# One statistic of the updated residual from sums taken early, one joint last down phase, and GpSimd adding every chunk

## The reference

```python
def _pre(x, g, mod, k):
    return _rmsnorm(x, g) * (1.0 + mod[:, 3 * k + 1][:, None]) + mod[:, 3 * k][:, None]
def _post(x, y, g, mod, k, weight):
    return x + weight * mod[:, 3 * k + 2][:, None] * _rmsnorm(y, g)
# a sub-layer
x = _post(x, _swiglu(_pre(x, g[0], mod_lat, 0), ffn1_gu[l], ffn1_down[l]), g[1], mod_lat, 0, 0.5)
```

## Time and profile before

| what | value |
|---|---|
| three runs | 2658.7, 2658.51, 2654.53 us; median 2658.51 |
| profiled execution, own time | 2659.8 us |
| its span, first to last instruction | 2658.0 us |
| PE busy | 2593.4 us (98%) |
| DVE busy | 1616.4 us (61%) |
| ACT busy | 714.7 us (27%) |
| POOL busy | 812.6 us (31%) |
| granted TensorE clock, mean | 0.995 |

### The profile page before, as it was taken

The page is one execution under the profiler, slowest core; times in us unless marked ns, Lnnn a source line. Parts: engine busy times, 40 slices in busy tenths (PEclk is TensorE's granted clock), DMA queues, the critical chain, the costliest instruction groups (busy, mean ns, idle before and its releaser), DMA issues.

```text
span 2658.0 us, 40824 instructions
## 1 busy us (share of the span) xinstructions
PE 2593.4 (98%) x17044; PEld 2436.5 (92%) x17044; DVE 1616.4 (61%) x2270; ACT 714.7 (27%) x1050; POOL 812.6 (31%) x1286
## 2 busy tenths in 40 slices
PE   6999999999999999999999999999999999999998
PEld 5999999998989899999999899999999878888886
DVE  6688878767574676676676633433434684544444
ACT  4222212123334411112212412112112424322222
POOL 1278876832140100000001248667551031000001
PEclk9999999999999999999999999999999999999999
DMA  9534544453464234434432422222223575233331
GB/s 336 153 124 157 157 143 134 159 181 124 124 193 143 81 95 134 135 111 130 133 105 86 112 68 82 94 96 87 93 96 125 175 195 159 72 96 95 95 95 64
DMA packets 340688, 334.55 MB, mean 126 GB/s; under 512 B 52496, under 2 KB 311704, under 8 KB 337432
## 3 DMA queue, kind: packets, MB, share of 16 engines
q1 hardware_dynamic: 278200, 198.19, 25.4%
q10 hardware_dynamic: 52288, 77.20, 8.7%
q0 software_dynamic: 10016, 56.56, 5.6%
HBM read 287.40 MB, written 44.50 MB: 125 GB/s over the span
## 4 chain that ended last, share of the span: by engine, by line
PE 84%; DVE 8%; DMA 2%; POOL 2%; issue 2%; ACT 1%; SPq 0%; DVEq 0%; POOLq 0%; ACTq 0%
PE ps L467 79%; POOL xT L1239 1%; DVE tmpN L1444 1%; DVE hL L1448 1%; DMA raw<-in_ffn_gu_dram 1%; PE ps L1259 1%; DMA adaW<-in_w_ada_dram 1%; ACT wH L452 1%; DVE zb L2075 1%; PE ps L1274 1%; DVE zd L2076 1%; PE ps L1004 1%; PE ps L1023 1%; DVE zc L2088 0%; DVE adaW L576 0%
## 5 line engine op out<-in xcount | busy, mean ns | idle before, releaser
L467 PE MATMUL ps<-hH,wH 128*128 128x384 f32 (+1 forms) x2928 | 1014.6, 347 | 8.8 <-DVE hL L1448 8.0
L467 PE MATMUL ps<-hH,wL 128*128 128x384 f32 (+1 forms) x2928 | 1005.5, 343 | 0.0
L467 PE MATMUL ps<-hL,wH 128*128 128x384 f32 (+1 forms) x2928 | 1005.4, 343 | 0.0
L459 DVE TENSOR_TENSOR wL<-raw,wH 128x1024 fp32r<-128x1024 f32 x300 | 389.5, 1310 | 477.0 <-ACT wH L452 475.5
L467 PEld LDWEIGHTS ps<-hH,wH 128*128 128x128 f32 x2928 | 550.5, 188 | 36.1 <-issue 7.4
L467 PEld LDWEIGHTS ps<-hH,wL 128*128 128x128 f32 x2928 | 550.6, 188 | 18.4
L467 PEld LDWEIGHTS ps<-hL,wH 128*128 128x128 f32 x2928 | 550.8, 188 | 18.0
L467 PE MATMUL ps<-midH,wH 128*128 128x384 f32 (+1 forms) x1232 | 424.8, 345 | 3.8 <-DVE yT L915 3.2
L452 ACT ACTIVATE wH<-raw 128x1024 fp32r<-128x1024 f32 x300 | 310.6, 1050 | 422.6 <-PE ps L467 407.4
L467 PE MATMUL ps<-midH,wL 128*128 128x384 f32 (+1 forms) x1232 | 422.2, 343 | 0.0
L467 PE MATMUL ps<-midL,wH 128*128 128x384 f32 (+1 forms) x1232 | 421.9, 342 | 0.0
(11 more groups left out here) (284 smaller groups left out, 2242.4 us busy)
## 6 DMA issues: line engine op xcount, KB each, us to landing
raw<-in_ffn_gu_dram SPq DMA_DIRECT2D x176, 512.0 KB, 3.9
adaW<-in_w_ada_dram ACTq DMA_DIRECT2D x40, 1536.0 KB, 7.1
raw<-in_ffn_down_dram SPq DMA_DIRECT2D x88, 512.0 KB, 3.5
x_d<-xT POOLq DMA_DIRECT2D x4, 3072.0 KB, 10.6
xT<-x_d POOLq DMA_DIRECT2D x4, 3072.0 KB, 11.3
ada_early<-in_w_ada_dram POOLq DMA_DIRECT2D x6, 1536.0 KB, 19.5
W_d<-gW POOLq DMA_DIRECT2D x16, 512.0 KB, 3.6
VT_d<-gVT ACTq DMA_DIRECT2D x16, 512.0 KB, 3.0
```

Source lines behind the costliest of these rows:

```text
L459: nc.vector.tensor_tensor(wL[:, n % SPLIT_SLOTS, :], raw[:, n % RAW_SLOTS, :], wH[:, n % SPLIT_SLOTS, :].bitcast(f32), ALU.subtract).then_ ...
L467: ins = nc.tensor.matmul(dst, a, b, start=first and n == 0, stop=last and n == 3 * len(pairs) - 1)
```

## The change

Between two sections the statistic of the new residual is no longer taken from the new `xT`. With z = coefP*y (per feature) and r = the reciprocal root of y's statistic (per token), the new x is x + r*z, and its sum of squares is sum x*x + 2r*sum x*z + r*r*sum z*z. sum x*x is kept from the last boundary (`sumX`). In the closing phase DVE makes x*z of every chunk (`cross_z`) behind each add, ACT makes z*z (`square_z`), GpSimd adds the z*z of chunks 0 to 5 (`sumZ`) beside the squares of y, and TensorE sums x*z over the partitions, for chunks 0 to 4 between the chunks (`cross_sums`). Three small sums on columns then give the new statistic (`new_sums`).

The scaling of `yT` is spread over the boundary and the first steps of the next section. ACT copies y's spread row from PSUM to an SBUF tile `rowY`, which chunks 1 to 7 read. GpSimd adds all 8 chunks to `xT`. An FFN's last two down phases become one over four middle blocks, with units of 4 blocks by 256 columns. The mixers begin with 3 units at once instead of 2. The section f21 keeps the old way of scaling, without a new statistic. At the start of the program two things move: ACT's and DVE's split of unit 2 stands later, and GpSimd's third to eighth early loads wait for unit 1 instead of 2.

```diff
-    def first_groups(pe, base, count, pre, between=None):
-        pe.wait_ge(w_lo, base + count)
+    def first_groups(pe, base, count, pre, between=None, cw_ready=None):
...
+            if k == 0:
+                pe.wait_ge(w_lo, base + u + 1)
+                if u == 1 and cw_ready:
+                    pe.wait_ge(cw, cw_ready)
+                if u == 2:
+                    pe.wait_ge(row_y, pre.after.nth + 1)
...
+    def cross_sums(pe, S, m):
+        pe.wait_ge(cross_x, KC * S.post.nth + m + 1)
+        return row_sums(pe, 7, crossed(S, m), S.tok0, TOK, m == 0, m == KC - 1)
...
+        summed = 0
+        for m in range(first, KC - 2):
+            pe.wait_ge(w_lo, S.wide + m // 2 + 1)
+            last_wait(pe, S, m)
+            signal(last_part(pe, S, m, moving, range(HC), (0, 1)), m)
+            while S.next and m >= 2 and summed < m:
+                cross_sums(pe, S, summed)
+                summed += 1
...
+            for m in range(2):
+                last_wait(pe, F, m)
+                for k in range(3):
+                    pe.wait_ge(mid_lo, F.n0["mid_lo"] + FC - 3 + k)
+                    last_part(pe, F, m, moving, (k,), (0, 1))
...
+    def last_adds(dve, S, ride=None):
...
+        for m in range(KC if S.tok0 else KC - 2):
+            last_ready(dve, S, m)
...
+            nc.vector.tensor_tensor(at, ps_pair(last_slot(S, m), S.tok0), at, ALU.add).then_inc(S.read, 1)
+            if S.next:
+                dve.wait_ge(S.read, S.read0 + m + 1)
+                cross_z(dve, S, m, token_segments(S.tok0), True)
+            if m % 2 and m < KC - 1:
+                split_lo(dve, S.wide + 3 + m // 2)
...
-    def add_squares(pool, N):
+    def add_squares(pool, N, S):
         for m in range(1, KC - 2):
-            pool.wait_ge(sq_y, KC * N.nth + m + 1)
+            for tile, squares_of, ready, done in ((sumY, lambda c: sq[:, c], sq_y, sum_y),
+                                                  (sumZ, lambda c: squared(S, c), sq_z, sum_z))[:2 if S.next else 1]:
...
-    def post_pool(pool, N):
+    def post_pool(pool, N, S):
         wait_back(pool, N)
-        for m in POOL_CHUNKS:
+        for m in range(KC if N.has_next else LAST_POOL):
...
+    def cross_z(dve, S, m, segments, done):
+        for t0, t1, v in segments:
+            ins = nc.vector.scalar_tensor_tensor(crossed(S, m)[:, t0:t1], yT[:, m, t0:t1], coefP[:, m, v:v + 1],
+                                                 xT[:, m, t0:t1], ALU.mult, ALU.mult)
...
+            row = seg_ps(4, 5, v) if m == 0 and N.has_next else rowY[:, t0:t1] if N.has_next else seg_ps(2, 3, v)
...
     def pre_vector(dve, N, late=()):
...
+            if post and m + 1 < KC and m + 1 >= AHEAD_Y:
+                scale_y(dve, post, m + 1)
...
-        first_groups(pe, M.base, 2, pre)
+        first_groups(pe, M.base, 3, pre, None, M.gen.n0["cw"] + 1)
...
-                pool.wait_ge(raw_ready[2], 16)
+                pool.wait_ge(raw_ready[1], 16)
```

More of the change, by code:

```diff
@@ L352, in make_ffn @@
         unit += 6 * (FC // 2)
-        F.late = [unit + 1, unit + 2]
+        F.late = [unit + 2]
         F.gen = Section("gen", GEN_COUNTS) if gen else None
@@ L866, in ffn_scalar @@
         load_root(act)
-        for m in range(KC if N.tok0 else KC - 2):
-            square_y(act, N, F, m)
-        if N.tok0 == 0:
-            square_last(act, N, F)
+        squares(act, N, F)
     def ffn_vector(dve, F):
@@ L902, in down @@
                     ada_steps(dve, following, m - (KC - AHEAD), m - (KC - AHEAD) + 1)
-                if last is not None and m < 4:
-                    ada_steps(dve, last, KC + 2 * m, KC + 2 * m + 2)
                 if m < KC - 1:
@@ L908, in down @@
                     dve.wait_ge(w_used, F.base + i + 2)
-                if last is not None and m == LAST_RIDE_CHUNK:
-                    take_columns_late(dve, last, 2 * tile_slot(F, g + m), TOK // 2)
                 if p == 0:
@@ L1340, in square_y, with squared, crossed, part_segments @@
         nc.scalar.activation(sq[:, m, N.tok0:TOK], yT[:, m, N.tok0:TOK], ACT.Square).then_inc(sq_y, 1)
+    def squared(S, m):
+        return zzF[:, m] if S.tag.startswith("f") else zzM[:, m]
+    def crossed(S, m):
+        return xzF[:, m] if S.tag.startswith("f") else xzM[m // HC][:, m % HC]
+    def part_segments(tok0, part):
+        if tok0:
+            return token_segments(tok0)
+        return [(0, CTX, CTXV), (CTX, HALF, LAT)] if part == 0 else [(HALF, TOK, LAT)]
+    def square_z(act, S, m, segments, done):
+        for t0, t1, v in segments:
+            ins = nc.scalar.activation(squared(S, m)[:, t0:t1], yT[:, m, t0:t1], ACT.Square, scale=coefP[:, m, v:v + 1])
+        if done:
+            ins.then_inc(sq_z, 1)
+    def cross_z(dve, S, m, segments, done):
+        for t0, t1, v in segments:
+            ins = nc.vector.scalar_tensor_tensor(crossed(S, m)[:, t0:t1], yT[:, m, t0:t1], coefP[:, m, v:v + 1],
+                                                 xT[:, m, t0:t1], ALU.mult, ALU.mult)
+        if done:
+            ins.then_inc(cross_x, 1)
+    def squares(act, N, S):
+        for m in range(KC if N.tok0 else KC - 2):
+            square_y(act, N, S, m)
+            if S.next:
+                square_z(act, S, m, token_segments(N.tok0), True)
+            if m % 2 and m < KC - 1:
+                split_hi(act, S.wide + 3 + m // 2)
+        if N.tok0 == 0:
+            square_last(act, N, S)
     def square_last(act, N, S):
@@ L1349, in square_last @@
             nc.scalar.activation(sq[:, m, HALF:TOK], yT[:, m, HALF:TOK], ACT.Square).then_inc(sq_y, 1)
+            square_z(act, S, m, part_segments(0, 1), True)
     def post_scalar(act, N, S):
-        root(act, rstd, N.tok0, N.nth, cols_y, sd_y)
+        root(act, rstd, rstd, N.tok0, cols_y, N.nth + 1, sd_y)
         for n in S.late:
             split_hi(act, n)
+        if S.next:
+            root(act, rstdX, sumX, N.tok0, sum_x, N.nth + 1, sd_x)
+            act.wait_ge(y_norm, KC * N.nth + 1)
+            for t0, t1, v in token_segments(N.tok0):
+                ins = nc.scalar.activation(rowY[:, t0:t1], seg_ps(4, 5, v), ACT.Copy)
+            ins.then_inc(row_y, 1)
     def square_x(act, N, wait_chunk):
@@ L1437, in build, with pre_vector, late_parts @@
     LATE_COEFS = {4: (5, 7), 7: (6, 8)}
-    def pre_vector(dve, N):
-        dve.wait_ge(bc_x if N.tok0 else bc_x_ctx, (N.nth if N.tok0 else N.ctx_nth) + 1)
+    def pre_vector(dve, N, late=()):
+        post = N.after
+        if N.tok0 == 0:
+            dve.wait_ge(bc_x_ctx, N.nth + 1)
+        else:
+            dve.wait_ge(bc_x, N.nth + 1)
         dsync(dve)
+        AHEAD_Y = 3
+        def late_parts():
+            for n in late:
+                split_lo(dve, n)
         def scaled(m, t0, t1, v):
@@ L2021, in mix_scalar @@
         load_root(act)
-        for m in range(KC if tok0 else KC - 2):
-            square_y(act, N, M, m)
-            if m % 2 and m < KC - 1:
-                split_hi(act, M.base + 17 + m // 2)
-        if tok0 == 0:
-            square_last(act, N, M)
+        squares(act, N, M)
     def by_chunk(t, m, tok0):
@@ L2357, in start_vector @@
                 inverse_x(dve, pres[0])
-        for n in range(SPLIT_SLOTS):
+        for n in range(2):
             split_lo(dve, n)
```

456 lines of the change are left out of this document (256 added, 200 removed).

## The result

The changed kernel takes 2690.42 us in the median of four runs (2689.62 to 2692.55), the kernel before 2656.88 us beside it (2654.53 to 2658.7): the ratio is 1.013, with a 95% interval from 1.0117 to 1.0142. I had said 2679 us, between 2645 and 2693. So the direction was right, and the loss is 33.5 us where I had worked out 20. The profiled execution's span went from 2658.0 to 2688.5 us.

A forecast was written before the change was run, and what follows sets the result against it. TensorE's list of matmuls, busy 98% of the span, was taken as the bound. Terms summed to +20.0 us on the profiled 2659.8, giving 2680; 2679 was said because that execution lies 1.3 above the median, range 2645 to 2693.

The forecast's parts named there:

- What two engines do to each other: DVE instructions with two SBUF operands and GpSimd instructions reading SBUF exclude each other; a 1.22 us split took 2.09.
- The boundary and the loop: After the last half add: first hL at 13.8 us, then 3.9 us a chunk; unit 0 at 40.2, three units 46.5.
- T1: Boundary from f10 to mixer m0, counted to the projection's unit 0 and the state-space matmuls: +5.6 us.
- T3: Boundary from f20 to f11: 85.4 us before, 87.8 after, so +2.4.
- T4: Boundary from f11 to mixer m1, like T1 without the pause in the closing phase of before: +8.2 us.
- The closing phase: Port work of 10.5 us a chunk pair against TensorE's 9.0; last half add at 40.1 us in mixers, 41.1 in FFNs.
- the rival in which the port is shared without idle time: DVE's and GpSimd's work interleave perfectly, last add at 37.2 us; total 2665 us, chance 0.15 for 2664 to 2671.
- T2: Boundary from mixer m0 to f20: 81.0 us before, 86.6 after, so +5.6.
- start 11.4 us behind it: In mixers the state-space matmuls start 11.4 us behind the projection's unit 0, now some 0.5 us sooner.
- between 0 and 3 us each, I take 1: Store of xT to DRAM now starts with the projection's stores and loads at T1 and T4: +2 us in all.
- The clock: Rival: new pauses slow matmuls four to eight times, up to 1.75 us each, up to 2693; 0.54 with the main forecast.
- Start and end: Start: a split leaves ACT's queue, early loads wait less, -2.5 us; end: f21's sums no longer late, -0.8 us.

The follow-up runs named there:

- e8: The kernel before with 90 additions, then 150 memsets that nobody reads, added on GpSimd in f20; 2719.29 us against 2654.48.
- e3: The changed kernel with GpSimd leaving the z*z of chunks 2 to 5 out of its sum; ratio to the kernel before 1.006.
- e7: e4 with hL of the chunk before ahead of tmpN ahead of mixers, and GpSimd's add of chunk m waiting for hL of chunk m-2; 2675.38 us, ratio 1.0072.
- e2: The changed kernel with unit 3 of the projection ahead of the first state-space matmuls in both mixers; ratio 1.0087.
- e4: The changed kernel with mixers beginning with 2 units again and scaling ahead of them reading y's row from PSUM; 2678.82 us, ratio 1.008.
- e1: The changed kernel with the mixers' store of xT waiting until the loads of projection units 0 and 1 have landed; ratio 1.0105.
- e6: The changed kernel with hL of the chunk before ahead of tmpN in the loop ahead of mixers, rowY still in SBUF; ratio 1.0138.
- e12: The kernel before with DVE's first rotation and scan in mixers ahead of two weight splits and the wait for xT's store; 2653.51 us, ratio 0.9988.

## Why the forecast was right, and where its size was not

**What two engines do to each other: right.** It decided the sign, and e8, e3 and e7 show it as a mechanism and not only as a coincidence of rows. Only its "only instructions with both operands in SBUF are held" was too narrow (last section).

**The boundary and the loop: right, nearly to the digit.** From the last half add at T1 (its end is 642.24): chunk 2 scaled at 10.75 us (forecast 11.0), first `hL` 13.6 (13.8), 3.93 us a chunk (3.9), unit 0 done 40.3 (40.2), three units 46.5 (46.5). At T3 the first matmul came 15.2 us behind the add. In e2, e3 and e4, which change nothing in the steps between T3's last half add and its first matmul, it is 13.6; in e1 and e6 it is 15.2 at T3 and 15.3 at T4. So this 1.6 us comes and goes between executions; why stays open.

**The closing phase: right in kind, too long for the mixer.** In FFNs 39.8 us at T1 and 40.2 at T3 and T4, from the last `midF` to the last half add, against 41.3 (41.1 and 0.2). In m0 the first add to the last half add took 33.64 us; my 40.1 less the first chunk's 4.2 and its start allowed 35.8. The "2.4 us idle" ahead of chunk 4's sum did not come there; TensorE's waits for x*z were 0.56, 0.11, 0.52 and 1.21 us at T1 to T4. My order of who takes the port left gaps that were filled, so in the mixer this term lies near the rival in which the port is shared without idle time; in FFNs it lies nearer my own. It is why T2 cost 3.4 and not 5.6.

**The state-space matmuls "start 11.4 us behind it", "some 0.5 sooner", and the spill, "between 0 and 3 us each, I take 1": the step that failed.** Unit 0 itself came somewhat sooner than forecast: its shift by ACT's copy is 4.7 us at T1 and 8.1 at T4, where the sums, before they take off the 0.5, have 6.1 and 8.7. But the distance behind it I put at 10.9 us, and 11.9 with the 1 us for the store of `xT` that had moved beside it; it became 15.0 and 13.6. e1 shows that the store made 4.0 us of it at T1. The bound of 3 us was too small, and I had worked it out from no row.

Of the 9 us that T1 and T4 took beyond the forecast, 2.9 are there when the state-space matmuls start (4.8 by this distance, less 2.0 by which unit 0 was sooner), 5.0 come in these matmuls, at half clock, and 1.1 behind them.

**The clock: nothing in the sum, and a rival that came in part, at another place.** The mean fell from 0.995 to 0.987. I had put its pauses into closing phases and behind the first chunk. In the closing phases ahead of T1 to T5 the granted clock stayed full. Around the first steps it was at half for 3.4 us at T1, T2 and T4 and for 10.2 in all at T3, which cost little, since DVE was behind: the loop turned in 3.93 us all the same. The half clock cost 2.4 and 2.5 us at the first state-space matmuls, and in m1 13.7 us at half clock followed the Tz wait, where the kernel before had 10.2. With e4 and e7, where no half clock followed that wait, the stretch from m1's channel matmuls to its last phase is 88.0 and 87.1 us, against 94.2 in the changed kernel and 92.4 before.

**Start and end: nothing, where I took -3.3.** The first matmul of f10 on weights came 0.41 us sooner, and by the end of f10 even that was gone. At the end the last row sum waits 0.87 us for ACT's square of the last chunk in the changed kernel; from the last matmul on both kernels are alike, so GpSimd's lateness had cost nothing.

**T3: right in part by luck.** The closing phase was 1.1 us shorter than forecast and the three units were done 48.0 us behind the last add, not 46.5; the two errors cancel in the +2.8. Its forecast was 3.2 less than T2's, for the pause and the slow matmuls in the closing phase of before; it came out 0.6 less. And e12, which does not touch that phase, took 36.78 us there instead of 38.37, without slow matmuls: 1.6 us of the 38.4 was the clock. What the joint last down phase gives by itself was not run and stays open, as do the split of e4's gain between its parts and z*z sums placed later on TensorE.
